# Exchanging the two inner loops of a weight slab in a matmul-bound encoder trunk: contraction tile outside, output tile inside

## The reference, cut to what matters

```
for layer in range(DEPTH):                        # 2
    hn = rms_norm(h, norm_mix_g[layer])
    if layer % 2 == 0:  h = h + even_mixer(hn, ...)   # FNet DFT + conformer conv, W_in, W_out
    else:               h = h + odd_mixer(hn, ...)    # gated short conv, W_in, W_out
    h = h + sq_relu_mlp(rms_norm(h, norm_mlp_g[layer]), mlp_w1[layer], mlp_w2[layer])
h = rms_norm(h, norm_final_g)
def sq_relu_mlp(xn, w1, w2):  return jnp.square(jax.nn.relu(xn @ w1)) @ w2
```

## Time and profile before

| what | value |
|---|---|
| time, median of 3 runs | 2116.27 us (2115.98 to 2116.4) |
| time of the profiled execution | 2116.13 us |
| its span | 2114.1 us |
| outside its span | 2.0 us |
| TensorE busy with matmuls | 2089.6 us (99%), 15226 matmuls |
| TensorE busy with weight loads | 1985.3 us (94%), 15226 loads |
| VectorE, ScalarE busy | 1281.1 us (61%), 927.1 us (44%) |
| mean granted TensorE clock | 0.998 |

### The profile page before, as it was taken

How to read it: one execution, slowest core, us unless ns; L and a number is a source line. 1 busy time by engine, 2 the same in 40 slices (tenths; PEclk the granted TensorE clock), 3 DMA queues, 4 the chain that set the end, 5 groups by cost and what they waited for, 6 DMA issues and landing times.

```text
span 2114.1 us, 36370 instructions
## 1 busy us (share of the span) xinstructions
PE 2089.6 (99%) x15226; PEld 1985.3 (94%) x15226; DVE 1281.1 (61%) x1300; ACT 927.1 (44%) x965; POOL 66.1 (3%) x40
## 2 busy tenths in 40 slices
PE   8999999999999999999999999999999999999997
PEld 8999999999999999999999999888888888888886
DVE  8999975545554554556566556665556555555555
ACT  6434464334434443445433334545335434434443
POOL 1001020000000000000100000010000000000001
PEclk9999999999999999999999999999999999999999
DMA  7442455555555555554555455455554554554552
GB/s 283 178 160 101 162 185 192 179 181 187 188 180 179 183 189 183 179 180 177 196 183 179 179 189 189 168 202 187 187 191 179 198 181 178 197 188 178 193 195 80
DMA packets 55336, 383.91 MB, mean 182 GB/s; under 512 B 6176, under 2 KB 8224, under 8 KB 9312
## 3 DMA queue, kind: packets, MB, share of 16 engines
q1 hardware_dynamic: 54880, 381.84, 50.1%
q0 software_dynamic: 240, 1.02, 0.1%
q10 hardware_dynamic: 144, 0.04, 0.0%
HBM read 380.78 MB, written 2.10 MB: 181 GB/s over the span
## 4 chain that ended last, share of the span: by engine, by line
PE 96%; DVE 2%; ACT 1%; issue 0%; DMA 0%; DVEq 0%; SPq 0%
PE banks L310 25%; PE banks L304 20%; PE banks L302 19%; PE banks L303 19%; PE banks L311 13%; DVE wl L796 1%; ACT wh L519 0%; DVE h L824 0%; ACT xs L536 0%; DMA raw<-weights 0%; DVE ssum L935 0%; DVE h L1149 0%; DVE h L1155 0%; ACT sq L546 0%; PE banks L437 0%
## 5 line engine op out<-in xcount | busy, mean ns | idle before, releaser
L796 DVE TENSOR_TENSOR wl<-raw,wh 128x1024 fp32r<-128x1024 f32 x720 | 891.9, 1249 | 720.6 <-ACT wh L519 719.5
L519 ACT ACTIVATE wh<-raw 128x1024 fp32r<-128x1024 f32 x720 | 753.9, 1058 | 971.3 <-PE banks L304 610.9
L302 PE MATMUL banks<-xs,wh 128*128 128x258 f32 (+1 forms) x2176 | 618.3, 284 | 10.3 <-DVE wl L796 10.3
L304 PE MATMUL banks<-xs,wl 128*128 128x258 f32 (+1 forms) x2176 | 621.1, 285 | 0.0
L303 PE MATMUL banks<-xs,wh 128*128 128x258 f32 (+1 forms) x2176 | 614.3, 282 | 0.0
L310 PE MATMUL banks<-hid,wh 128*128 128x512 f32 x1280 | 448.5, 395 | 0.0
L302 PEld LDWEIGHTS banks<-xs,wh 128*128 128x128 f32 x2176 | 412.4, 190 | 10.6 <-issue 8.8
L303 PEld LDWEIGHTS banks<-xs,wh 128*128 128x128 f32 x2176 | 411.4, 189 | 0.1
L304 PEld LDWEIGHTS banks<-xs,wl 128*128 128x128 f32 x2176 | 409.9, 188 | 0.0
L304 PE MATMUL banks<-hid,wl 128*128 128x258 f32 x1280 | 363.8, 284 | 0.0
L302 PE MATMUL banks<-hid,wh 128*128 128x258 f32 x1280 | 361.9, 283 | 1.4 <-DVE hid L840 1.4
(11 more groups left out here) (103 smaller groups left out, 779.5 us busy)
## 6 DMA issues: line engine op xcount, KB each, us to landing
raw<-weights SPq DMA_DIRECT2D x359, 1024.0 KB, 4.8
out<-h SPq DMA_DIRECT2D x8, 256.0 KB, 2.7
h<-x SPq DMA_DIRECT2D x3, 544.0 KB, 10.6
raw<-weights SPq DMA_DIRECT2D x2, 512.0 KB, 6.0
conv<-dft_seq POOLq DMA_DIRECT2D x1, 580.5 KB, 13.2
h<-x SPq DMA_DIRECT2D x2, 272.0 KB, 4.3
act<-dft_ch POOLq DMA_DIRECT2D x1, 258.0 KB, 7.9
par<-params POOLq DMA_DIRECT2D x1, 160.0 KB, 6.4
```

The costliest lines, as they stand in the source:

```text
L302: pe.matmul(dst, w[0], v[0], start=start, stop=False)
L304: return pe.matmul(dst, w[1], v[0], start=False, stop=stop)
L519: act.activation(wh[:, j % RING, :, :], src.rearrange("p (t c) -> p t c", t=SLAB_K), ACT.Copy).then_inc(high_ready, 1)
L796: dve.tensor_tensor(wl[:, j % RING, :, :], src.rearrange("p (t c) -> p t c", t=SLAB_K), wh[:, j % RING, :, :].bitcast(F32), ALU.subtract). ...
```

## The change

The two loops inside a slab are exchanged. Before, the four output tiles `m` were outside and the two contraction tiles `t` inside, so that both contraction tiles of a bank were issued one after the other: six matmuls of `product` (four of `wide_product`) into a bank, then the next bank. After, `t` is outside and `m` inside: three matmuls (two) into a bank, then the next, and the four banks are visited twice per slab. The number of matmuls and weight loads, their operands, the `start` and `stop` flags of each bank, the waits at the head of a slab and the signal at its end are the same. The last matmul of a slab is still that of `m` = 3, `t` = 1.

```
-                    for m in range(M):
-                        for t in range(SLAB_K):
+                    for t in range(SLAB_K):
+                        for m in range(M):
                             k = tile0 + SLAB_K * s + t
                             slot = (ring0 + s) % RING
                             cols = slice(P * m, P * m + P)
```

## The result

The changed kernel takes 2126.39 us (median of 5 runs, 2126.13 to 2126.65) against 2115.98 us (5 runs, 2114.93 to 2116.4) for the kernel before: ratio 1.005, 95% interval 1.0038 to 1.0062. It is 10.4 us slower, 0.5%. The span of the profiled execution went from 2114.1 to 2124.4 us, so all of it lies inside the program.

A forecast was written before the change was run, and what follows sets the result against it. The prediction took TensorE's matmul pace as the bound, not weight supply or bank reading. Every term was 0 us, so 2116.13 + 0 gave 2116.1 us profiled, 2116.3 us against the median; range 2102 to 2131 us.

The forecast's parts named there:

- outcome slower by over 0.2%: Whole kernel: chance 0.29, summed from 0.23 for dear bank changes, 0.05 for a slower rhythm and 0.01 for the clock.
- Supply, signals, bank times, weight loads at 0 us each: Slab loops: same waits and signals, unnoticed shifts in first and last bank writes, loads indifferent to block order; 0 us each.
- 0 ns per change of bank: Slab loops: eight bank changes per slab instead of four, 2880 added, taken at 0 ns each, with -8 and +5 as range.
- the 5 ns between two L310 matmuls: Wide stage: first L310 matmul into a bank 397 ns, second 392; as bank-change cost, an upper bound of 14.4 us.
- The -8 ns from the sequence DFT: Last sequence DFT: 18 matmuls per bank at 120.3 ns against 119.4 with six; lower bound per change, -13.8 us.
- the rival of the dear bank change: First matmul into a bank, now also for tile 1: 5 ns per change, +14.4 us, 2130.7 us; chance 0.23 including wide-only form.
- the rhythm: All 15226 matmuls: another operand order may shift the mean 0.5 ns either way, 2108.7 or 2123.9 us; chance 0.10.
- The pace from 258 to 272 columns: Matmul streams: pace rises 5.9 ns, 0.42 ns per column; carried to a mean of 384 columns it gives 172.3 ns.
- the 2.6 ns: Wide stage: rest between 172.3 ns extrapolated and 174.9 measured; as bank-change cost 31 ns each, which the prediction ruled out.
- What would show it: Signs if right: three stretches keep 798, 6030 and 3888 matmuls within 0.2%, TensorE waits some 13 us, tile 0 stays longer.
- The line for slower: Sign of a slower outcome: all L310 matmuls at 397 ns and more, fewer than 3870 matmuls in the third stretch.
- The clock: TensorE: more bank changes might risk the full clock; a tenth of matmuls at half level adds 157 us, 2273 us; chance 0.01.

The follow-up runs named there:

- Destination alone: Kernel before with only the bank order exchanged (next bank with each product), weights and activations read as before: 2116.21 us against 2116.15 us, ratio 1.0.

## Why the prediction was right or wrong

**The number.** 2116.3 us and no change were forecast, with a chance of 0.54; 2126.4 us is inside the range of 2102 to 2131 us but outside the forecast's own 2113 to 2119. The outcome slower by over 0.2% had 0.29. That the range held the time is luck: its upper end was the price of the bank changes, and these cost nothing.

**Supply, signals, bank times, weight loads at 0 us each:** right. The waits are the same, and weights read in the new order alone gave a ratio of 1.0.

**0 ns per change of bank:** right. Destination alone gave 1.0 (0.999 to 1.0009). Neither bound was the cost of a bank change: the 5 ns between two L310 matmuls stayed in alternation when every product went to a new bank (destination alone), and moved to other positions once the tile order changed. The -8 ns from the sequence DFT compared streams that differ in start addresses, rows and operands too; its 120.3 ns lies among the paces that other start addresses alone gave (118.3 to 120.6 ns), but what makes it so is not shown. That one of the two bounds times the added changes (14.4 us) came near the loss of 10.4 us was chance; on the time alone the rival of the dear bank change could have looked confirmed.

**The step that failed** is that the sum had no term for the order of the streamed tiles. The prediction named "the rhythm", a pipeline that beats against the order of operands, only as a rival with a chance of 0.10, and priced it at 0.5 ns per matmul for all 15226, 2123.9 us if slower. A change of pace by the order of operands is what happened, with +0.56 ns in 9216 matmuls, +1.22 ns in 4608 and nothing in the rest. What the rival says of operands is shown, for the streamed ones alone; that a pipeline is the reason is not. Its price of 0.5 ns was a guess, near the measured one with 258 columns and too small by more than half in the wide stage. The rows had the clue: durations that repeat with a period of two products in a stream whose addresses repeat with the same period. It was read as "moves the 5 ns and adds none".

**The pace from 258 to 272 columns.** The prediction divided windows by their counts, edges included. From starts the paces are 119.4, 125.6 and 175.0 ns (68.80 and 72.32 us / 576, 67.20 us / 384). The slope is then 0.44 ns per column and gives 119.4 + 126 x 0.44 = 174.8 ns for the wide stage, so most of the 2.6 ns that the prediction discussed as the possible price of a bank change was a reading error. Its choice of 0 was right.

**What would show it.** The counts to within 0.2% failed (6002 against 6030 is 0.46%, 3861 against 3888 is 0.69%). The line for slower asked for all L310 matmuls at 397 ns and fewer than 3870 in the third stretch: the count came, the durations came for six of eight only, and that remainder was the first sign that banks were not the reason.

**The clock.** The granted clock stayed at 1.00 in all stretches, and TensorE was busy without a gap in them (680.00 of 680.00 us), with eight bank changes per slab as with four. The Trainium skill, page "TensorE: Matmul & The Clock Gate", section "A second HAM failure mode: psum-queue depth-cycling", tells of brief idle times between groups of matmuls in a kernel that cycled through banks. This trace has the cycling without the idle times, and no swing of the clock.

**Left open.** Shown is that the sequence of start addresses of the streamed operand changes the pace with all else alike, and that tiles at one address modulo 256 make both orders equal. Not shown is which part of the chip makes it so, whether accesses of other engines to the same memory take part, what selects between two paces of one order, and which sequence is best. Nor is it shown why the 272-column stage is immune to the exchange (798 and 799). It is not immune to addresses: 24 of its slabs took 72.32 us with both orders, and 72.45 us with both orders once `xs` was padded to 2304 bytes.

## What to carry to other kernels

When TensorE streams without a gap as here, its pace can still depend on the start addresses of the streamed operand in their order, by about a per cent at most in these kernels; a reordering of loops that leaves every count alone can win or lose that. Before blaming the destination, split the reordering into destination, weights and activations: three kernels with mixed results tell more than any single row. And read pace not as busy share, which was 99% throughout, but as matmuls per long stretch of time, where a thousandth shows, or better as the time between two starts that lie many slabs apart: 10 ns in 69 us.

## What the runs showed of the hardware that was not expected

- Changing the PSUM bank with every product, eight times in a slab of 16 or 24 matmuls, was free: 6030 and 3888 matmuls as with four changes.
- Moving the start of the streamed high part by 56 bytes to a multiple of 64 made the 258-column stream slower: 5966 matmuls in 310 to 1030 us against 6030.
- A tile distance of a multiple of 256 bytes was slower than one by which the starts alternate by 128 modulo 256: 398 matmuls in 70 us of the wide stage against 402 in the kernel before (1570 to 1640 us).
- One order of reads had at least two stable paces in one execution, 120.0 and 118.3 ns, and its runs spread over 13 us, where the kernel before spreads over 2 us. The pace changed where a sum over partitions broke into the stream, at 1038.93 us.
- The pace is steady to half a cycle of 1.2 GHz per slab over 24 slabs, so a change of a few cycles in 3440 can be read from one trace: 3440 cycles before and 3456 changed, 3452 and 3460 with tiles 2240 bytes apart.
